# Roots of the norms on ScalarE with scale and epsilon in the same operation, and a spare root ahead of them

## The chip, the core and the metric

The kernel is one program on one core of a Trainium2 chip. The core has a matrix engine (TensorE, PE in the rows), a vector engine (VectorE, DVE), a scalar engine that evaluates functions from tables (ScalarE, ACT), GpSimd (POOL) and SyncE (SP), whose queue issues most of the DMAs. The engines run their own instruction streams and wait for each other by semaphores. The metric is the device time of one execution in microseconds, the median of several runs; lower is better. All data is float32. The engine PE works on operands rounded to a shorter format, so each product is made of three passes: high by high, high by low and low by high.

## What is computed

A stack of three layers. A diffusion-like block of two layers works on 256 latent and 256 context rows of width 1024; a third layer (sparse attention, retention, gated feed-forward) follows on the 256 latent rows. What matters here are the norms:

```python
def rms_norm(x, g):
    y = xf * lax.rsqrt(jnp.mean(xf * xf, axis=-1, keepdims=True) + NORM_EPS)   # 1e-6
    return y * g
...
for i in range(2):
    u = modulate(h, g_pre_mix[i], ...)            # rms_norm(h, gain) * (1 + scale) + shift
    o = even_mixer(u) or odd_mixer(u)             # recurrence + attention, output projection
    h = h + gate * rms_norm(o, g_post_mix[i])
    f = sqrelu_mlp(modulate(h, g_pre_ff[i], ...), w_ff1[i], w_ff2[i])
    h = h + gate * rms_norm(f, g_post_ff[i])
...
yn = (y - mu) * lax.rsqrt(var + GN_EPS) ...       # even layer, per head of 64, GN_EPS = 64e-5
q, k = rms_norm per head of 64                    # odd layer, attention D
o_r = (o - mean) * lax.rsqrt(var + EPS) * w       # third layer, retention, per head of 256
return rms_norm_2(x, norm_final_w)
```

## The kernel before

**The plan.** One Python list, `plan`, is written in the order in which the stages are composed: `step(name, ...)` adds an entry, and generators are advanced in turns to interleave independent work. Then each engine goes through the whole list and emits what it has under each name; an engine that has nothing under a name skips it. So the order on each engine's queue is the order of the plan, and between engines only semaphores order the work (`at(...)` names a point, `wait_ge` waits for points; `ve.last()` and `sc.last()` are the engine's own last instruction). PSUM banks are handed out with `take` and `give`. A queue is in order: what stands behind a waiting instruction waits too.

**Weights.** `cols` declares a chunk of 1 MB: SP loads it into a slot of a ring (L2896), ACT copies it into a window as the rounded high part (`split`, L2448, 128x2048), and DVE subtracts to get the low part (L1869). `chunk` puts the split of each chunk at the place in the plan where the chunk before it was declared, one chunk ahead of its use. PE then multiplies in three passes (L1377 to L1379).

**Norms.** `normed(T, k)` is the norm of tile k (128 rows) in stage T. Its steps: for the norms behind a projection, `residual` (the root of the projected row's mean square, then h + gate * o / rms); `square` (ACT squares and sums H, L2489, with an instruction that reads the accumulator behind it); `diag` (DVE scales and adds epsilon, L1894; ACT takes the root, L2493; DVE takes the reciprocal, L1896, and writes a diagonal matrix, L1901); `x` (PE multiplies the tile by the diagonal, which turns and normalises it, L1442; DVE, L1913 or L1915, and ACT, L2502, copy the result out with gain and shift); `x hi` (ACT, L2448, 128x512) and `x lo` (DVE, L1920). With this the next matrix product can start. The stages are m0 (start), f0 (behind mix0, four tiles), m1 (behind ff2 of layer 0, four tiles), f1 (behind mix1, two tiles), m2 (behind ff2 of layer 1, two), u (third layer, two) and the final norm. A "seam" is the stretch from the end of one product to the start of the next, with such a norm between.

**Projections.** `out_proj` makes the output in two halves of 512 columns, c = 0 and 1. For each half ACT squares and sums the result per tile into `SSQ[:, m, c]` (L2515), and DVE multiplies it by the gate (L1942; L1936 and L1939 where it also adds to an earlier part). In the last chunk of c = 1 the tiles are finished one by one, and the steps of `normed` are advanced, one per generator, between tiles. `residual` on DVE first adds the two sums (L1925), then scales and adds epsilon (L1894), waits for ACT's root (L2493), takes the reciprocal and forms the new h (L1928).

**Other roots.** The recurrence's head norm (`gn var`: DVE L2182 from PSUM, ACT L2643 in place), the query and key norm of the odd layer (`d var`: DVE L2256, ACT L2703), the retention norm (DVE L2368, ACT L2816), the final norm (L1894, L2493), and `prep norm` (L2615), which isn't touched.

A root needs its table on ACT. The load (ACT_TABLE_LOAD) isn't in the source: it is put ahead of the first function whose table isn't the active one, and 36 of them are in the program. Exp, Sigmoid, Silu and Gelu need other tables; Copy, Identity and Square go with any.

## Time and profile before

| | |
|---|---|
| median of 3 runs | 2102.7 us (2098.2 to 2103.3) |
| profiled execution | 2100.6 us, span of its instructions 2098.8 us |
| PE busy | 1863.1 us, 89% |
| weight load of PE busy | 1558.0 us, 74% |
| DVE busy | 1109.6 us, 53% |
| ACT busy | 886.5 us, 42% |
| POOL busy | 214.4 us, 10% |
| chain that ended last | PE 75%, DVE 10%, ACT 6%, issue 2%, POOL 2%, SP queue 2%, DMA 2% |
| mean granted clock of PE | 0.948 of full speed |

The page's chain is to be read as the time that would go if its link were faster: PE's 75% are matrix products, and the 16% of DVE and ACT are links between them. Busy shares of DVE and ACT are averages over stages in which they matter and stages in which they don't.

### The profile page before, as it was taken

The page shows a single profiled execution, that of the slowest core. Times are in us where ns is not written, and L with a number is a line of the kernel's source. Part 1 is how long each engine was busy: PE and PEld are TensorE (multiplying, and loading weights), DVE is VectorE, ACT ScalarE, POOL GpSimd, SP SyncE. Part 2 cuts the span into 40 slices and gives each one's busy share as a digit, 9 for nine tenths or more (in the row PEclk, how much of TensorE's full clock was granted, in tenths as well). Part 3 has the DMA queues.
Part 4 walks back from the last instruction along what each step waited for, and adds up shares of the span by engine and source line. Part 5 has one row for each costly group of instructions (what it writes and reads, how often), then busy time and mean ns, then how long its engine had stood idle before and what let it go on. Part 6 is the DMA issues. An engine that isn't in the chain of part 4 may idle for free.

```text
span 2098.8 us, 40122 instructions
## 1 busy us (share of the span) xinstructions
PE 1863.1 (89%) x16962; PEld 1558.0 (74%) x16962; DVE 1109.6 (53%) x1711; ACT 886.5 (42%) x1423; POOL 214.4 (10%) x214
## 2 busy tenths in 40 slices
PE   5899779888898889999997799799979999679996
PEld 3776568777787688888876676698877677569985
DVE  1457564565545554224344765565445574556863
ACT  2336544353431444214224256564332465346652
POOL 0000035334342000000000100010000000000210
PEclk9999889999999999999998899899989999789998
DMA  8233232222231312233323310365534534134552
GB/s 268 92 121 109 77 121 85 87 91 91 83 103 42 121 61 92 90 100 101 101 80 58 133 61 25 103 186 190 186 108 148 169 98 151 65 124 161 181 163 99
DMA packets 201377, 237.19 MB, mean 113 GB/s; under 512 B 14347, under 2 KB 158573, under 8 KB 201197
## 3 DMA queue, kind: packets, MB, share of 16 engines
q1 hardware_dynamic: 195856, 227.33, 34.2%
q10 hardware_dynamic: 5341, 7.30, 1.0%
q8 instruction: 133, 2.18, 0.4%
q14 instruction: 47, 0.39, 0.1%
HBM read 233.56 MB, written 1.05 MB: 112 GB/s over the span
## 4 chain that ended last, share of the span: by engine, by line
PE 75%; DVE 10%; ACT 6%; issue 2%; POOL 2%; SPq 2%; DMA 2%; ACTq 0%; DVEq 0%; POOLq 0%
PE bank L1377 17%; PE bank L1378 17%; PE bank L1379 17%; PE bank L1569 9%; ACT window L2448 2%; SPq L2896 2%; DVE window L1869 2%; PE bank L1557 2%; PE bank L1536 2%; PE bank L1548 2%; PE bank L1428 1%; PE bank L1442 1%; DVE window L1920 1%; PE bank L1754 1%; PE bank L1576 1%
## 5 line engine op out<-in xcount | busy, mean ns | idle before, releaser
L1377 PE MATMUL bank<-window 128*128 128x512 f32 (+1 forms) x2136 | 762.8, 357 | 55.1 <-DVE window L1920 29.6
L1378 PE MATMUL bank<-window 128*128 128x512 f32 (+1 forms) x2136 | 749.8, 351 | 0.0
L1379 PE MATMUL bank<-window 128*128 128x512 f32 (+1 forms) x2136 | 749.0, 351 | 0.0
L1869 DVE TENSOR_TENSOR window<-arena,window 128x2048 fp32r<-128x2048 f32 (+1 forms) x164 | 372.1, 2269 | 271.5 <-ACT window L2448 269.7
L1377 PEld LDWEIGHTS bank<-window 128*128 128x128 f32 x2136 | 415.5, 195 | 119.0 <-DVE window L1920 30.7
L2448 ACT ACTIVATE window<-arena 128x2048 fp32r<-128x2048 f32 (+3 forms) x292 | 377.1, 1291 | 211.0 <-PE bank L1379 123.5
L1379 PEld LDWEIGHTS bank<-window 128*128 128x128 f32 x2136 | 415.2, 194 | 51.3
L1378 PEld LDWEIGHTS bank<-window 128*128 128x128 f32 x2136 | 416.0, 195 | 48.2 <-issue 0.2
L2448 ACT ACTIVATE arena<-bank 128x256 f32<-128x256 f32 (+1 forms) x298 | 127.0, 426 | 367.1 <-PE bank L1379 128.6
L1569 PE MATMUL bank<-arena 64*64 64x64 f32 (+1 forms) x5888 | 215.2, 228 | 18.8 <-DVE arena L1363 10.2
L1569 PEld LDWEIGHTS bank<-arena 64*64 64x64 f32 x5888 | 201.8, 137 | 35.6 <-DVE arena L1363 11.9
L2842 POOL TENSOR_TENSOR arena<-arena 128x256 f32<-128x256 f32 x80 | 67.8, 848 | 409.9 <-ACT arena L2448 303.6
L2658 ACT ACTIVATE arena<-bank 128x512 f32<-128x512 f32 (+1 forms) x64 | 31.4, 491 | 152.8 <-PE bank L1379 151.5
L2561 ACT ACTIVATE arena<-bank,arena 128x512 f32<-128x512 f32 (+3 forms) x112 | 58.5, 522 | 56.5 <-DVE arena L2016 35.2
L2072 DVE TENSOR_TENSOR arena<-arena,bank 128x512 f32<-128x512 f32 (+1 forms) x80 | 50.7, 634 | 58.8 <-PE bank L1569 57.4
L1442 PE MATMUL bank<-extra,arena 128*128 128x128 f32 x288 | 48.2, 342 | 35.4 <-DVE extra L1901 35.4
L1442 PEld LDWEIGHTS bank<-extra,arena 128*128 128x128 f32 x288 | 46.0, 253 | 38.8 <-DVE extra L1901 38.8
L2210 DVE TENSOR_TENSOR arena<-arena 128x512 f32<-128x512 f32 (+1 forms) x48 | 29.0, 603 | 84.9 <-ACT arena L2658 84.4
L1428 PE MATMUL bank<-arena 128*32 128x256 f32 x768 | 58.8, 426 | 13.3 <-DMA arena<-in_w_ada 13.3
L2016 DVE TENSOR_REDUCE arena<-bank 128x1 f32<-128x512 f32 (+4 forms) x96 | 51.7, 539 | 23.4 <-PE bank L1540 17.0
L2864 POOL TENSOR_TENSOR arena<-arena 128x2048 f32<-128x2048 f32 x2 | 9.0, 4510 | 487.2 <-DMA arena<-in_c_rpb 487.1
L2448 ACT ACTIVATE extra<-bank 128x512 f32<-128x512 f32 (+2 forms) x96 | 46.9, 489 | 19.2 <-PE bank L1548 16.6
(283 smaller groups left out, 1674.8 us busy)
## 6 DMA issues: line engine op xcount, KB each, us to landing
arena<-in_w_ff SPq DMA_DIRECT2D x64, 1024.0 KB, 5.4
arena<-in_w_ada SPq DMA_DIRECT2D x48, 1024.0 KB, 5.6
arena<-in_w_in SPq DMA_DIRECT2D x23, 1024.0 KB, 5.1
arena<-in_w_ffn_up SPq DMA_DIRECT2D x22, 1024.0 KB, 5.0
arena<-in_w_ffn_down SPq DMA_DIRECT2D x10, 1024.0 KB, 5.1
arena<-in_w_in_even SPq DMA_DIRECT2D x9, 1024.0 KB, 5.5
arena<-in_w_out SPq DMA_DIRECT2D x8, 1024.0 KB, 5.2
arena<-in_w_in_odd SPq DMA_DIRECT2D x8, 1024.0 KB, 6.9
```

What stands on the lines that cost most here:

```text
L1377: e.matmul(o, rr(l[0]), rr(r[0]), start=start, stop=False)
L1378: e.matmul(o, rr(l[0]), rr(r[1]), start=False, stop=False)
L1379: return e.matmul(o, rr(l[1]), rr(r[0]), start=False, stop=stop)
L1428: t = e.matmul(u.b[q:q + 32, 0:256], SV[:, k, :], w.v[:, k, :], start=k < 4, stop=k >= 4)
L1442: t = e.matmul(u.b[:, j * 128:j * 128 + 128], H[:, k, (q + j) * 128:(q + j) * 128 + 128], DIAG[:, k, :], start=True, stop=True)
L1569: t = e.matmul(o[h0:h1, c], l[i][h0:h1, c], r[i][h0:h1, c], start=i == 0, stop=i == len(l) - 1)
L1869: e.tensor_tensor(rr(raw), raw, rr(w.high, F32), SUB).then_inc(*ve.tick(w.ready))
L2016: e.tensor_reduce(low[:, h * ns:h * ns + ns], b, AX.X, MAX, negate=True).then_inc(*ve.tick(at("max", S, i, h)))
L2072: e.tensor_tensor(w, w, x, SUB).then_inc(*ve.tick(b.empty, at("w", *u)))
L2448: return e.activation(o, i, ACT.Copy, **k)
L2561: e.activation(a.P[i % a.NP][h][:, s * n:s * n + n], u.b[:, s * n:s * n + n], ACT.Exp, bias=low[:, x:x + 1], accum_out=total[:, x:x + 1]). ...
L2842: return e.tensor_tensor(z.L[l % 2], z.G[:, :, 0], lvl[:, 1 - d, l:l + 1, :].to_broadcast([128, NCH, 64]), MUL)
```

## The change

ACTIVATE computes func(scale * in + bias). The change lets ACT do the scaling and the adding of epsilon inside the root, with scale as an immediate and bias as a column of memory: `eps` (1e-6) and `eps_gn` (64e-5), two columns of `tiny` that DVE sets at the start.

- `square` on ACT is followed at once by the root (`root`), so the root moves from step `diag` to step `square`; DVE's `diag` keeps reciprocal and diagonal.
- `residual`: DVE scales the first half's sum and adds epsilon in `out block` of c = 1 (`first squares`, RS[:, m, 3]); ACT takes the root of the second half's sum with that column as bias. DVE's addition of the sums and its scaling go.
- `gn var`, `d var`, `ret norm` and the final norm: DVE's instruction goes; for the first two ACT reads PSUM itself and frees the bank.
- `root table`: a root of `eps` into a spare column, at the start (behind `silu`, ahead of the loads of h on ACT's queue) and in `out_proj` ahead of c = 1. Where another table is active there, the load stands with it; elsewhere only the spare root is added.

```diff
@@ out_proj
         for c in range(2):
+            if c and (then or not gate):
+                step("root table")
             for m in range(ntok):
@@ start
     step("silu")
+    step("root table")
@@ vector
-        def rstd(acc, var, inv, summed, rooted):
-
-            ve.wait_ge(ve.last(), *([at(*summed)] if summed else []))
-            e.tensor_scalar(var, acc, 1.0 / 1024, 1e-6, MUL, ADD).then_inc(*ve.tick(at("var", *rooted)))
+        def inverse(k, *rooted):
+
             ve.wait_ge(ve.last(), at(*rooted))
-            e.reciprocal(inv, var).then_inc(*ve.tick(at("inv", *rooted)))
+            e.reciprocal(RS[:, k, 2:3], RS[:, k, 1:2]).then_inc(*ve.tick(at("inv", *rooted)))
@@ residual on DVE
-            ve.wait_ge(ve.last(), at("out squares", p.of, k))
-            e.tensor_reduce(RS[:, k, 0:1], SSQ[:, k, :], AX.X, ADD).then_inc(*ve.tick())
-            rstd(RS[:, k, 0:1], RS[:, k, 1:2], RS[:, k, 2:3], None, ("res root", T, k))
+            inverse(k, "res root", T, k)
@@ out_block on DVE
+            if p.gate and c:
+                ve.wait_ge(ve.last(), at("out square", name, 0, m))
+                e.tensor_scalar(RS[:, m, 3:4], SSQ[:, m, 0:1], 1.0 / 1024, 1e-6, MUL, ADD).then_inc(*ve.tick(at("first squares", name, m)))
@@ gn_var and d_var on DVE
-            e.tensor_scalar(pA[:, p, :], u.b[:, :], 1.0 / 64, 64e-5, MUL, ADD).then_inc(*ve.tick(u.empty, at("y var", p)))
-            e.tensor_scalar(TMP[x % 3][:, 0:n], u.b[:, 0:n], 1.0 / 64, 1e-6, MUL, ADD).then_inc(*ve.tick(u.empty, at("d var", x)))
@@ square, residual and root table on ACT
             e.activation(JUNK, H[:, k, :], ACT.Square, accum_out=RS[:, k, 0:1]).then_inc(*sc.tick(at("squared", T, k)))
-
-        def root(a, *key):
-            sc.wait_ge(sc.last(), at("var", *key))
-            e.activation(a, a, ACT.Sqrt).then_inc(*sc.tick(at(*key)))
+            sc.wait_ge(sc.last(), at("eps"))
+            e.activation(RS[:, k, 1:2], RS[:, k, 0:1], ACT.Sqrt, scale=1.0 / 1024, bias=eps).then_inc(*sc.tick(at("root", T, k)))
+
+        def residual(T, k):
+            p = norms[T]
+            sc.wait_ge(sc.last(), at("out squares", p.of, k), at("first squares", p.of, k))
+            e.activation(RS[:, k, 1:2], SSQ[:, k, 1:2], ACT.Sqrt, scale=1.0 / 1024, bias=RS[:, k, 3:4]).then_inc(*sc.tick(at("res root", T, k)))
+
+        def root_table():
+            sc.wait_ge(sc.last(), at("eps"))
+            e.activation(spare_root, eps, ACT.Sqrt).then_inc(*sc.tick())
@@ gn_var and d_var on ACT
-            sc.wait_ge(sc.last(), at("y var", p))
-            e.activation(pA[:, p, :], pA[:, p, :], ACT.Sqrt).then_inc(*sc.tick(at("y root", p)))
+            u = bank("var", p)
+            sc.wait_ge(sc.last(), u.full)
+            e.activation(pA[:, p, :], u.b[:, :], ACT.Sqrt, scale=1.0 / 64, bias=eps_gn).then_inc(*sc.tick(u.empty, at("y root", p)))
-            sc.wait_ge(sc.last(), at("d var", x))
-            e.activation(a, a, ACT.Sqrt).then_inc(*sc.tick(at("d root", x)))
+            u, n = bank("d sums", x), d_parts[x][2]
+            sc.wait_ge(sc.last(), u.full)
+            e.activation(TMP[x % 3][:, 0:n], u.b[:, 0:n], ACT.Sqrt, scale=1.0 / 64, bias=eps).then_inc(*sc.tick(u.empty, at("d root", x)))
```

ACT from the end of mix1's c = 0 to the norm f1, before. L2515 squares the projection, L2448 128x2048 is the split of a chunk, L2493 a root, L2489 the square of h, L2502 the copies of x.

```order
L2515 ACTIVATE extra,arena<-bank 128x512 x2
L2448 ACTIVATE window<-arena 128x2048 x2
L2515 ACTIVATE extra,arena<-bank 128x512
L2493 ACT_TABLE_LOAD
L2493 ACTIVATE arena<-arena 128x1
L2515 ACTIVATE extra,arena<-bank 128x512
L2493 ACTIVATE arena<-arena 128x1
L2489 ACTIVATE extra,arena<-arena 128x1024 x2
L2493 ACTIVATE arena<-arena 128x1 x2
L2502 ACTIVATE arena<-bank,arena 128x128 x8
L2448 ACTIVATE window<-arena 128x4x128 x4
```

The same place after. L2516 is the projection's square, L2442 the split, L2494 the spare root, L2490 the residual's root, L2483 and L2485 the square of h and its root, L2503 the copies of x.

```order
L2516 ACTIVATE extra,arena<-bank 128x512 x2
L2494 ACT_TABLE_LOAD
L2494 ACTIVATE arena<-arena 128x1
L2442 ACTIVATE window<-arena 128x2048 x2
L2516 ACTIVATE extra,arena<-bank 128x512
L2490 ACTIVATE arena<-arena 128x1
L2516 ACTIVATE extra,arena<-bank 128x512
L2490 ACTIVATE arena<-arena 128x1
L2483 ACTIVATE extra,arena<-arena 128x1024
L2485 ACTIVATE arena<-arena 128x1
L2483 ACTIVATE extra,arena<-arena 128x1024
L2485 ACTIVATE arena<-arena 128x1
```

The table load moved from behind the two splits to ahead of them, with the spare root; each root of a norm now stands right behind its square, so that the root of tile 0 is ahead of the square of tile 1.

DVE at the same place, before: L1869 low parts of two chunks, L1942 the gate product, L1925 the sum, L1894 scaling, L1896 reciprocal, L1928 the new h, L1901 a diagonal.

```order
L1869 TENSOR_TENSOR window<-arena,window 128x2048 x2
L1942 TENSOR_TENSOR arena<-bank,arena 128x512
L1925 TENSOR_REDUCE arena<-arena 128x1
L1894 TENSOR_SCALAR arena<-arena 128x1
L1896 RECIPROCAL arena<-arena 128x1
L1928 SCALAR_TENSOR_TENSOR arena<-arena 128x1024
L1942 TENSOR_TENSOR arena<-bank,arena 128x512
L1925 TENSOR_REDUCE arena<-arena 128x1
L1894 TENSOR_SCALAR arena<-arena 128x1
L1896 RECIPROCAL arena<-arena 128x1
L1928 SCALAR_TENSOR_TENSOR arena<-arena 128x1024
L1894 TENSOR_SCALAR arena<-arena 128x1
```

After: L1875 low parts, L1938 the first squares, L1947 the gate product, L1900 reciprocal, L1930 the new h, L1905 a diagonal.

```order
L1875 TENSOR_TENSOR window<-arena,window 128x2048 x2
L1938 TENSOR_SCALAR arena<-arena 128x1
L1947 TENSOR_TENSOR arena<-bank,arena 128x512
L1900 RECIPROCAL arena<-arena 128x1
L1930 SCALAR_TENSOR_TENSOR arena<-arena 128x1024
L1938 TENSOR_SCALAR arena<-arena 128x1
L1947 TENSOR_TENSOR arena<-bank,arena 128x512
L1900 RECIPROCAL arena<-arena 128x1
L1930 SCALAR_TENSOR_TENSOR arena<-arena 128x1024
L1900 RECIPROCAL arena<-arena 128x1
L1905 TENSOR_SCALAR extra<-arena 128x128
L1900 RECIPROCAL arena<-arena 128x1
```

The addition and the scaling between gate product and reciprocal are gone, also the scaling ahead of each diagonal's reciprocal; one scaling of the first half's sum stands ahead of each gate product.

## Rows read from the trace of the kernel before

**Rows 1.** Waits of PE: us in total, times, longest
```profile
PE bank L1442 <- DVE extra L1901: 35.4, 11, 7.5
PE bank L1377 <- DVE window L1920: 29.6, 6, 5.9
```

**Rows 2.** ACT timeline at seam m2: start, duration, line, instruction, idle before
```profile
1522.02 0.60 ACT L2515 ACTIVATE extra<-bank 128x512 f32<-128x512 f32 x1 [6.22 <-PE bank L1379]
1524.74 0.60 ACT L2515 ACTIVATE extra<-bank 128x512 f32<-128x512 f32 x1 [0.56 <-PE bank L1379]
1528.84 1.06 ACT L2489 ACTIVATE extra<-arena 128x1024 f32<-128x1024 f32 x1 [0.50 <-DVE arena L1928]
1530.02 0.20 ACT L2493 ACTIVATE arena<-arena 128x1 f32<-128x1 f32 x1
```

**Rows 3.** DVE timeline at seam m2
```profile
1522.81 0.69 DVE L1942 TENSOR_TENSOR arena<-bank,arena 128x512 f32<-128x512 f32 x1 [4.62 <-ACT extra L2515]
1523.54 0.15 DVE L1925 TENSOR_REDUCE arena<-arena 128x1 f32<-128x2 f32 x1
1523.72 0.15 DVE L1894 TENSOR_SCALAR arena<-arena 128x1 f32<-128x1 f32 x1
1524.28 0.16 DVE L1896 RECIPROCAL arena<-arena 128x1 f32<-128x1 f32 x1 [0.40 <-ACT arena L2493]
1527.46 1.28 DVE L1928 SCALAR_TENSOR_TENSOR arena<-arena 128x1024 f32<-128x1024 f32 x1
1530.32 0.16 DVE L1896 RECIPROCAL arena<-arena 128x1 f32<-128x1 f32 x1 [1.39 <-ACT arena L2493]
```

**Rows 4.** PE timeline at seam m2
```profile
1530.86 6.57 PE L1442 MATMUL bank<-extra,arena 128*128 128x128 f32 x32 [6.22 <-DVE extra L1901]
```

**Rows 5.** Groups of ACT instructions by shape: busy us, mean ns
```profile
L2448 ACT ACTIVATE arena<-bank 128x512 f32<-128x512 f32 x60 | 35.8, 597 | 151.9 <-PE bank L1379 110.4 <-PE bank L1569 24.9 <-PE bank L1451 16.0
L2561 ACT ACTIVATE arena<-bank,arena 128x512 f32<-128x512 f32 x48 | 33.0, 689 | 27.9 <-DVE arena L2016 19.1 <-DVE arena L2019 5.2 <-DVE arena L2021 2.4
```

**Rows 6.** ACT timeline, a table load behind a copy
```profile
1772.71 1.28 ACT L2757 ACT_TABLE_LOAD   x1
1774.00 3.63 ACT L2757 ACTIVATE arena<-arena 128x4096 f32<-128x4096 f32 x1
```

**Rows 7.** ACT and PE timelines in mix1 and seam f1
```profile
1310.59 3.87 ACT L2448 ACTIVATE window<-arena 128x2048 fp32r<-128x2048 f32 x2
...
1320.02 1.28 ACT L2493 ACT_TABLE_LOAD   x1 [1.25 <-DVE arena L1894]
...
1314.49 0.39 PE L1379 MATMUL bank<-window 128*128 128x512 f32 x1
1314.95 0.50 PE L1377 MATMUL bank<-window 128*128 128x512 f32 x1
```

**Rows 8.** DVE and PE timelines at seam f0
```profile
734.97 0.16 DVE L1896 RECIPROCAL arena<-arena 128x1 f32<-128x1 f32 x1 [1.06 <-ACT arena L2493]
...
741.98 0.58 PE L1377 MATMUL bank<-window 128*128 128x256 f32 x1 [4.42 <-DVE window L1920]
```

**Rows 9.** DVE and SP timelines at the end of seam m1
```profile
1123.00 4.32 DVE L1920 TENSOR_TENSOR window<-arena,window 128x512 fp32r<-128x512 f32 x6
...
1127.40 21.74 SPq L2896 DMA_DIRECT2D arena<-in_c_rpb  x32
```

**Rows 10.** Waits of PE from 1188 to 1216 us
```profile
PE bank L1518 <- DVE arena L2266: 1.9, 1, 1.9
PE bank L1377 <- DVE window L1869: 0.9, 1, 0.9
```

**Rows 11.** DVE and ACT timelines, last variance and final norm
```profile
671.43 0.69 DVE L2182 TENSOR_SCALAR arena<-bank 128x512 f32<-128x512 f32 x1 [2.01 <-PE bank L1687]
...
2087.64 1.28 ACT L2493 ACT_TABLE_LOAD   x1 [0.34 <-DVE arena L1894]
```

**Rows 12.** Busy time by stretch, behind seam f0: columns PE PEld DVE ACT POOL, clock
```profile
742.00:750.00 8.00, 8.00 (x44) 8.00 (x45) 5.37 (x7) 2.64 (x3) 0.00 (x0) 0.62 0.00 0
```

More of the change, by code:

```diff
@@ L180, in program @@
     tiny = sb(64)
+    eps, eps_gn, spare_root = [tiny[:, i:i + 1] for i in (63, 62, 61)]
     ident = sb(128)
@@ L2366, in ret_norm @@
         def ret_norm():
-            ve.wait_ge(ve.last(), *[at("ret squared", h, i) for h in range(4) for i in range(2)])
-            e.tensor_scalar(a1, a1, 1.0 / 256, 1e-6, MUL, ADD).then_inc(*ve.tick(at("ret var")))
             ve.wait_ge(ve.last(), at("ret root"))
@@ L2416, in final @@
             a, b, r = [tiny[:, 4 * k + i:4 * k + i + 1] for i in range(3)]
-            rstd(a, b, r, ("final squared", k), ("final root", k))
+            ve.wait_ge(ve.last(), at("final root", k))
+            e.reciprocal(r, b).then_inc(*ve.tick())
             ve.wait_ge(ve.last(), at("spread", ("final",), 0))
@@ L2802, in final @@
             e.activation(junkf, H[:, k, :], ACT.Square, accum_out=a).then_inc(*sc.tick(at("final squared", k)))
-            root(tiny[:, 4 * k + 1:4 * k + 2], "final root", k)
+            sc.wait_ge(sc.last())
+            e.activation(tiny[:, 4 * k + 1:4 * k + 2], a, ACT.Sqrt, scale=1.0 / 1024, bias=eps).then_inc(*sc.tick(at("final root", k)))
         steps = {"load h": load_h, "more columns": more_columns, "silu": silu, "mod": mod, "split": split, "spread": spread,
-                 "square": square, "diag": lambda T, k: root(RS[:, k, 1:2], "root", T, k), "x": norm_x, "x hi": x_hi,
-                 "residual": lambda T, k: root(RS[:, k, 1:2], "res root", T, k), "out block": out_block,
+                 "square": square, "root table": root_table, "x": norm_x, "x hi": x_hi,
+                 "residual": residual, "out block": out_block,
                  "even start": even_start, "kB": kB_, "vB": vB_, "pA": pA_, "pA gates": pA_gates, "scores": scores, "turn p": turn_p,
@@ L2814, in scalar @@
                  "kv": kv_, "vsw": vsw_, "gt": gt_, "gelu": gelu, "vg": vg, "merge start": merge_start, "ret o": ret_o,
[L2815 to L2816 removed]
+                 "ret square": ret_square, "ret norm": lambda: (sc.wait_ge(sc.last()),
+                                                               e.activation(a1, a1, ACT.Sqrt, scale=1.0 / 256, bias=eps).then_inc(*sc.tick(at("ret root")))),
                  "ret turn": ret_turn, "z turn": z_turn_, "up": up, "gated": gated, "final": final,
```

17 lines of the change are left out of this document (5 added, 12 removed).

## The prediction

> **What bounds the kernel now.** I read the page first, then the waits of PE, then the chain of waits, and last the timelines of ACT, DVE and PE at the places where the chain leaves PE. In the waits of PE the reader is to see two releasers ahead of all others: the diagonal that DVE writes from 1/rms, and the low half of the normalised x [rows 1]. Together they cost PE 65 us. They belong to six "seams", places where one matrix product ends and the next can't begin before the rows are normalised: m0 at the start, f0 and m1 with four tiles, f1, m2 and u with two. At a seam the chain runs through ACT and DVE by turns, in instructions of 0.15 to 1.3 us with a hop between engines, so every one that goes from it shortens the kernel. Between seams PE is the bound, and an edit there is worth nothing unless ACT or DVE is late.
>
> **The seam in full: m2, tiles 0 and 1.** Before: ACT squares tile 0 at 1522.02 [rows 2]; DVE multiplies by the gate until 1523.50, adds the two sums (1523.54), scales and adds epsilon (1523.72), waits 0.40 us for the root, takes the reciprocal at 1524.28 [rows 3]. After: root 0 stands behind its own square on ACT (0.68 us for square and accumulator read, then the root), done at 1523.0 beside the gate product, so the reciprocal follows at 1523.53: 0.75 us earlier. Tile 1's square is released by PE at 1524.74 [rows 2] and doesn't move; its reciprocal comes behind the gate product at about 1526.24, the residual product (1.28 us) ends at 1527.72 instead of 1528.74. DVE has one small instruction more there, the first squares (0.15 us as the scaling of the same shape, with a gap 0.19), but it lies in the wait for that square.
> The order gives more than the removed instructions. Before, ACT does square 0, square 1, root 0, root 1; root 0 starts at 1530.02, behind square 1 which waited for the second residual, and DVE idles 1.39 us before reciprocal 0 [rows 2, 3]. After, root 0 follows square 0 and is done near 1527.2. Reciprocal and diagonal of tile 0 then wait only for DVE's own residual product: 1527.75 + 0.19 + 0.29 = 1528.23, PE starts at 1528.28 and not at 1530.86 [rows 4]. That is 2.6. Tile 1's diagonal is ready near 1529.8, before PE has done tile 0's sixteen matmuls (half of 6.57 us [rows 4]), so PE doesn't stop again. Less 0.25 for the spare root of this projection: **2.3 us**.
>
> **Price of the new forms.** No root of before has a bias from memory. ACTIVATE on 128x512 from PSUM is 597 ns as a copy and 689 ns with such a bias [rows 5], so I add 0.09 us to each root (0.20 to 0.29); from below it is 0, from above 0.1. The Trainium skill, page "ScalarE: Activation LUTs", section "What ACT_TABLE_LOAD costs", says each [128,1] pointer operand adds about 93 ns; by that rule, the trace agrees, and it speaks mildly against the change, which gives 42 roots such an operand. A table load takes 1.28 us; where one stands right behind a copy (no idle time is put before it, at 1772.71) the next ACTIVATE begins at 1774.00, nothing between [rows 6]. So a spare root with its load is 1.28 + 0.20 + two gaps = **1.54 us** of ACT, one without load 0.25. The same section puts a drain of about 1380 ns on each switch; the rows show none, and if it appeared where a load is moved to, f1 would be worth 1.4 us less.
> The loads stay as many as they were (36); three are moved: at m0, before mix1's second half, before down's second half.
>
> **f1 (behind mix1).** The same walk as m2 gives its 2.6, and the load of 1.28 us, which stands at 1320.02 between the scaling and root 0 with nothing beside it [rows 7], is gone from there: 3.9 us. But the load isn't gone. It now stands on ACT in front of the split of 1310.59, and that split is itself on the chain: PE finished the chunk before it and started at 1314.95, 0.46 us behind the start of the last matmul where 0.23 is the rule [rows 7]. No slack, so all 1.54 us come back as a wait of PE. Net **2.4**. What is queued behind the load: two splits, the second for the first feed-forward chunk, which has the whole seam as slack.
>
> **f0 and m1 (four tiles).** By the same walk the residual products come 0.75 us earlier at tile 0 and 0.55 more for each further tile (0.74 less the 0.19 of the first squares, which here stand between busy DVE instructions). Then the order: at f0 DVE waits 1.06 us for the last root, which stands on ACT behind copies of x and splits, and all low halves come behind it [rows 8]. After, tile 0's diagonal is ready at 721.95, PE takes 3.7 us for its sixteen matmuls, and from 725.7 on ACT runs without a gap: copies of x of tile 0 (1.93), square and root of tile 3 (1.5, done at 729.1), copies of tile 1, high half of tile 0 (1.29), copies of tile 2, high half of tile 1, which ends at 735.7; DVE, no longer held by the root, has tile 1's low half ready at 736.5, and PE starts there and not at 741.98: 5.4. At m1 the last low halves end at 1127.3 (1123.00 + 4.32), and SP starts the 32 loads of the bias right behind, 21.7 us ahead of the weights of the odd layer [rows 9]; so m1's end passes to all that follows through SP. After, by the same walk (tile 0's diagonal at 1102.1, tile 1's at 1106.6, ACT without a gap from 1110.2), ACT's last high half ends at 1121.4 and DVE at 1122.1: 5.2. Lower end of each is the removed instructions alone, 0.74 + 3 x 0.55 + 0.25 = 2.6. A four-tile walk has many joints, so I take **5.0 and 4.9**.
>
> **Query and key norm of the odd layer.** The variance leaves DVE. Its last two instructions stood on DVE behind a copy that waits for a matrix product, while ACT sat idle; ACT now takes those roots straight from PSUM, and the split queued behind them comes earlier too, as do DVE's low half and reciprocals. PE has two waits there that hang on it, 0.9 and 1.9 us [rows 10]: both go, **2.8**, from below 0 if the copy or the weights hold the split anyway.
>
> **The rest.** u: root 0 before square 1: **1.1**, from the same order. Recurrence: the last variance, 0.69 us on DVE with nothing beside it [rows 11], is taken by ACT: **0.7**; the other three lie in a stretch where PE is busy: 0 to 2.1, I take 0.5. Retention norm: a hop and a small instruction, **0.2**. Final norm: the load of 1.28 us goes from the end of the kernel [rows 11] and two hops of 0.24; its spare root stands before a split with about 1.0 us of slack, so 0.5 comes back: **1.3**. m0: the chain runs on loads of w_ada and w_in_even; four roots earlier are hidden by them: 0; the spare root stands ahead of the loads of h, which are wanted 20 us later.
>
> **Sum.** 2.3 + 2.4 + 5.0 + 4.9 + 2.8 + 1.1 + 0.7 + 0.5 + 0.2 + 1.3 = 21.2. The profiled execution took 2100.6 (span 2098.8), so 2079.4; the median of the runs shown lies 2.1 above it: **2081.5 us**, 1.0% faster. Its own range: with the odd layer at 0 and f0 and m1 half way to their lower ends it is 2087; with all of the recurrence's 2.1, the full walks and a little clock it is 2076.
>
> **Rivals.**
> A. Only the removed instructions count, since at each seam the next thing (ACT's copies of x, a split, PE's own slow matmuls) is late in the place of the root. Then f0 and m1 give 2.6 each, f1 1.2, m2 1.3, u 0.25, the odd layer 0, final 1.3, the rest 0.9: 10 us, **2092**. For it: ACT is nearly full in the second half of f0 and m1. Against: at m2 and f1 both engines stand idle for over 1 us, waiting for that root [rows 2, 3].
> B. The seams become short enough that PE's clock isn't lowered behind some of them. After f0's seam, in which PE was mostly idle, the granted clock was 0.62 over 8 us: the lower level, 1.2 GHz, for most of it [rows 12], some 3.0 us lost. Spared at three of the five seams: **2073**. Against: at m2 PE would still be idle for some 3.6 us, and most of the time behind that.
> C. Slower. Four lanes share DVE's, ACT's and POOL's queues in the recurrence (245 to 645 us). Three instructions fewer on DVE move the phase of the lanes, and each of the 16 units could find one engine taken. The gains elsewhere are paid back if a unit loses 1.3 us (21.2/16); at 1.9 us, 30 us are lost: **2112**. It is one mechanism, but a queue that is emptier usually lets the next in sooner, and DVE is busy only a good half of the time there, by the page's slices.
> D. The change doesn't do what it says: the moved loads hurt at mix1 and down, the seams keep their length because the trace's hops are shorter with the new waits than I think: **2100**.
>
> **Chances.** Forecast 0.62, A 0.23, B 0.08, C 0.03, D 0.04. A measurement of this kernel tells some 0.3% (6 us) from no change: faster 0.93, within it 0.04, slower 0.03. The range holds the forecast's own and reaches to A and B: 2073 to 2094.
>
> **What would show it.** In the trace after: each root at 0.29 us right behind its square; PE's waits for the diagonal and the low half down from 65 to some 45 us; at mix1 a table load before a split and a new wait of PE for the low half of weights near 1.5 us; no load in the last 12 us; SP's bias loads starting some 12 us earlier by the span; no wait of PE for the key norm. I am wrong if m1's end moves less than 3 us against m1's start, if the recurrence's length changes by more than 3 us, or if PE's first matmul behind a seam is released by something new.

## The result and the profile after

The changed kernel takes 2072.9 us (median of 4 runs, 2072.2 to 2077.4) against 2102.0 us before: ratio 0.987, 95% interval 0.9857 to 0.9883. That is 29 us, 1.3 to 1.4% faster, where the forecast was 2081.5 us and its range 2073 to 2094. The direction and most of the waits were as forecast, but the time is 8.6 us below the forecast and stands at the lower end of the range (0.1 us under it). Of the 8.6, 7.0 are missing in the sum (28.2 us gained by the spans, 21.2 forecast); the other 1.6 come from the medians, which lay 2.1 us above the profiled execution before and 0.5 after. The profiled span went from 2098.8 to 2070.6 us, and its mean granted clock from 0.948 to 0.954.

The waits of PE, after (us in total, times, longest). The diagonal (line 1905 now) holds PE for 18.0 us instead of 35.4, the low half of x (line 1924) for 28.8 instead of 29.6 [rows 1]. Together that is 46.8 where 45 was expected. The third row, the low half of weights (L1875), was 16.6 before, and the new wait at mix1 is in it.

```profile
PE bank L1381 <- DVE window L1924: 28.8, 6, 5.7
PE bank L1381 <- DVE window L1875: 19.0, 9, 5.0
PE bank L1446 <- DVE extra L1905: 18.0, 9, 4.4
```

Seam m2 on ACT, answering to [rows 2]: start, duration, line, instruction, idle before. L2516 is the square of the projection, L2490 the residual's root, L2483 and L2485 the square of h and its root, L2503 the copies of x.

```profile
1500.64 0.60 ACT L2516 ACTIVATE extra<-bank 128x512 f32<-128x512 f32 x1 [6.22 <-PE bank L1383]
1501.14 0.19 ACT L2516 ACTIVATION_READ_ACCUMULATOR extra<-bank 128x1 f32 x1
1501.36 0.29 ACT L2490 ACTIVATE arena<-arena 128x1 f32<-128x1 f32 x1
1503.36 0.60 ACT L2516 ACTIVATE extra<-bank 128x512 f32<-128x512 f32 x1 [1.70 <-PE bank L1383]
...
1504.41 1.06 ACT L2483 ACTIVATE extra<-arena 128x1024 f32<-128x1024 f32 x1
1505.37 0.19 ACT L2483 ACTIVATION_READ_ACCUMULATOR extra<-arena 128x1 f32 x1
1505.59 0.29 ACT L2485 ACTIVATE arena<-arena 128x1 f32<-128x1 f32 x1
1506.45 1.06 ACT L2483 ACTIVATE extra<-arena 128x1024 f32<-128x1024 f32 x1 [0.57 <-DVE arena L1930]
```

Each root takes 0.29 us and stands right behind its square. Root 0 (1505.59) is ahead of square 1 (1506.45), where before it stood behind it. On DVE, answering to [rows 3], nothing is left between gate product (L1947) and reciprocal (L1900), and the 1.39 us of idle time before reciprocal 0 are gone:

```profile
1504.15 0.69 DVE L1947 TENSOR_TENSOR arena<-bank,arena 128x512 f32<-128x512 f32 x1 [0.32 <-ACT extra L2516]
1504.88 0.16 DVE L1900 RECIPROCAL arena<-arena 128x1 f32<-128x1 f32 x1
1505.08 1.28 DVE L1930 SCALAR_TENSOR_TENSOR arena<-arena 128x1024 f32<-128x1024 f32 x1
1506.39 0.16 DVE L1900 RECIPROCAL arena<-arena 128x1 f32<-128x1 f32 x1
1506.59 0.29 DVE L1905 TENSOR_SCALAR extra<-arena 128x128 f32<-128x128 f32 x1
```

PE, answering to [rows 4]: the wait is 3.67 us instead of 6.22, which is the 2.6 of the walk. But the 32 matmuls themselves now take 5.28 us instead of 6.57, and nothing was removed from them:

```profile
1506.93 5.28 PE L1446 MATMUL bank<-extra,arena 128*128 128x128 f32 x32 [3.67 <-DVE extra L1905]
```

The same line by its instructions, over seams f1 and m2, of before and then of after. The three numbers are the shortest, the median and the longest duration in ns:

```profile
L1442 PE MATMUL bank<-extra,arena x64: 275/421/582, 1328.2 to 1537.2; 128*128 128x128 f32 x64
```
```profile
L1446 PE MATMUL bank<-extra,arena x64: 274/306/579, 1308.1 to 1511.9; 128*128 128x128 f32 x64
```

The matmuls that lasted 275 ns ran at the higher clock level; at the lower one most lasted some 420, and the 580 are the first ones behind a wait. What counts for the time is how far apart they start: 0.21 us at the lower level (24 of them in 5.12 us from 1531.45 on, before) and 0.11 at the higher (12 in 1.33 us from 1510.05 on, after). The granted clock over the 32 was 0.56 before and 0.71 after. This is the part that the forecast's sum left out.

mix1 after, on ACT and then on PE. The spare root's load (L2494) stands ahead of two splits, and PE gets a wait of 1.30 us that [rows 7] don't have:

```profile
1292.80 1.28 ACT L2494 ACT_TABLE_LOAD   x1
1294.10 0.20 ACT L2494 ACTIVATE arena<-arena 128x1 f32<-128x1 f32 x1
1294.33 3.86 ACT L2442 ACTIVATE window<-arena 128x2048 fp32r<-128x2048 f32 x2
...
1298.70 0.50 PE L1381 MATMUL bank<-window 128*128 128x512 f32 x1 [1.30 <-DVE window L1875]
```

The other places: PE's first feed-forward product of f0 (answers to [rows 8]); SP's loads of the bias, 12.0 us earlier than in [rows 9]; ACT's root of the last variance straight from PSUM, and the last root of the kernel, which has no load before it (both answer to [rows 11]).

```profile
735.74 0.58 PE L1381 MATMUL bank<-window 128*128 128x256 f32 x1 [4.42 <-DVE window L1924]
...
1115.39 20.08 SPq L2899 DMA_DIRECT2D arena<-in_c_rpb  x30
...
671.76 0.69 ACT L2645 ACTIVATE arena<-bank,arena 128x512 f32<-128x512 f32 x1 [1.28 <-PE bank L1691]
...
2065.67 0.30 ACT L2806 ACTIVATE arena<-arena 128x1 f32<-128x1 f32 x1
```

**Where the time went.** Both kernels issue the same 16962 matmuls in the same order, so the start of the i-th can be taken from either trace and subtracted. What is gained in a stretch has two parts: PE waits less (no matmul runs), or the same matmuls take less time, which is how TensorE's clock shows. Over the whole kernel the second part is the difference of PE's busy time, 1863.1 us before and 1859.6 after. "with fillers" is the gain between two kernels of the experiments with filler matmuls in their seams (below). The stretches end at 671, 713, 1090, 1167, 1300, 1515, 1700 and 2000 us of the trace before. In us gained:

| stretch | forecast | measured | of it waits | of it matmul time | with fillers |
|---|---|---|---|---|---|
| recurrence | 0.5 | -0.3 | 2.0 | -2.3 | 0.9 |
| last variance | 0.7 | 0.7 | 0.7 | -0.1 | 0.7 |
| f0 | 5.0 | 7.1 | 4.1 | 3.1 | 5.7 |
| m1 | 4.9 | 4.9 | 6.1 | -1.1 | 5.4 |
| odd layer's key and query norm | 2.8 | 5.1 | 2.8 | 2.3 | 3.9 |
| mix1 and f1 | 2.4 | 3.9 | 2.8 | 1.1 | 3.9 |
| m2 | 2.3 | 5.3 | 3.4 | 1.8 | 4.0 |
| retention, u | 1.3 | 0.3 | 1.3 | -1.0 | 0.9 |
| down, final norm | 1.3 | 1.3 | 1.6 | -0.3 | -0.1 |
| sum | 21.2 | 28.2 | 24.7 | 3.5 | 25.3 |

The waits of down and final norm hold the 2.1 us gained behind the last matmul. (The ends of matmuls are modelled in the profile, so the split into the two parts is less sure than their sum.) The repetition of the changed kernel has nearly the same waits in most places (m2 2.6, m1 5.7, the others within 0.5) but other matmul times at f1 (-0.2) and m2 (4.3): the clock's part of a single seam differs by 1 to 2.5 us between two traces of the same code, its sum outside the recurrence less (5.8 us here, 7.0 in the repetition).

The recurrence scatters from trace to trace by more than the change could do there: up to its last matmul the delay against before was 0.3 us in the first trace of the changed kernel, 0.7 in its second, -0.4 in a variant that leaves the recurrence's code alone, and 1.5 in another. Its -2.3 us of matmul time can't be laid to the change of its variances, since the kernel with these put back has -2.5.

### The profile page after: what moved, and what is told of

It is laid out like the page before. It is cut to its first block, busy times and chain, and to the rows that moved or that the text cites. A ratio compares the mean times of both kernels' runs of the same rounds, so it can differ in the third digit from the quotient of the medians.

```text
span 2070.6 us, 40061 instructions
## 1 busy us (share of the span) xinstructions
PE 1859.6 (90%) x16962; PEld 1554.9 (75%) x16962; DVE 1097.0 (53%) x1671; ACT 892.2 (43%) x1430; POOL 214.7 (10%) x214
## 4 chain that ended last, share of the span: by engine, by line
PE 77%; DVE 9%; ACT 5%; POOL 2%; SPq 2%; issue 2%; DMA 2%; ACTq 0%; DVEq 0%; POOLq 0%
PE bank L1381 18%; PE bank L1383 17%; PE bank L1382 17%; PE bank L1573 9%; ACT window L2442 2%; SPq L2899 2%; DVE window L1875 2%; PE bank L1561 2%; PE bank L1540 2%; PE bank L1552 2%; PE bank L1432 1%; PE bank L1446 1%; PE bank L1758 1%; PE bank L1580 1%; PE bank L1544 1%
## 5 line engine op out<-in xcount | busy, mean ns | idle before, releaser
L1381 PE MATMUL bank<-window 128*128 128x512 f32 (+1 forms) x2136 | 761.0, 356 | 56.6 <-DVE window L1924 28.8
L1875 DVE TENSOR_TENSOR window<-arena,window 128x2048 fp32r<-128x2048 f32 (+1 forms) x164 | 372.1, 2269 | 273.5 <-ACT window L2442 271.7
L2442 ACT ACTIVATE window<-arena 128x2048 fp32r<-128x2048 f32 (+3 forms) x292 | 377.1, 1291 | 209.8 <-PE bank L1383 121.7
L2442 ACT ACTIVATE arena<-bank 128x256 f32<-128x256 f32 (+1 forms) x298 | 127.3, 427 | 368.6 <-PE bank L1383 130.1
L2442 ACT ACTIVATE extra<-bank 128x512 f32<-128x512 f32 (+2 forms) x96 | 47.0, 489 | 19.4 <-PE bank L1552 16.8
```

What stands on the lines that cost most here:

```text
L1381: e.matmul(o, rr(l[0]), rr(r[0]), start=start, stop=False)
L1875: e.tensor_tensor(rr(raw), raw, rr(w.high, F32), SUB).then_inc(*ve.tick(w.ready))
L2442: return e.activation(o, i, ACT.Copy, **k)
```

## The experiments

All kernels of one comparison ran on the same chip, with runs of the kernel before among them (medians 2100.8 to 2101.7).

**The changed kernel again**, as the base of the first comparison.

> The changed kernel once more, as the yardstick of this call. Both theories: 2073 us, ratio to the kernel before 0.987; f0's first feed-forward matmul about 7 us earlier than in the kernel before, the odd layer's key norm about 5 us.

Measured: 2072.4 us, ratio 0.9861 (0.9846 to 0.9876), span 2071.1. The gain repeats, with 5.9 us at f0's first product (about 7 expected) and 5.3 in the odd layer.

**Root of the square back behind the next square** (the new form, the old order).

```diff
             e.activation(JUNK, H[:, k, :], ACT.Square, accum_out=RS[:, k, 0:1]).then_inc(*sc.tick(at("squared", T, k)))
+
+        def root(T, k):
             sc.wait_ge(sc.last(), at("eps"))
...
-                 "square": square, "root table": root_table, "x": norm_x, "x hi": x_hi,
+                 "square": square, "diag": root, "root table": root_table, "x": norm_x, "x hi": x_hi,
```

> The changed kernel with each square's root put back behind the next square (same instruction forms, same number, old place in ACT's order). Theory 1 (the order on ACT is a large part of the gain): slower than the changed kernel by 1.6 us at f1 and m2 each, 0.9 at u, 2 to 3 at f0 and m1 each, 9 us in all, plus 2 to 3 us where PE's lower clock stretches come back: 2082 to 2085. Theory 2 (only the removed instructions count): within 1 us of the changed kernel.

Measured: 2083.0 us, ratio 0.9903 (0.9887 to 0.992), 10.6 above the control. PE's wait for the diagonal is back at 27.6 us:

```profile
PE bank L1381 <- DVE window L1924: 29.2, 6, 5.7
PE bank L1446 <- DVE extra L1905: 27.6, 11, 5.3
```

So over a third of the gain is the place of an instruction in ACT's queue and not the instructions saved, within theory 1's 2082 to 2085. By stretch, against the trace of the changed kernel, it is 2.5 us at f0, 0.8 at m1, 3.1 at mix1 and f1, 4.0 at m2 and 0.2 at u, where theory 1 had 1.6 at f1 and m2 each and 2 to 3 at m1. It is a matter of waits: between matmuls PE stands idle 11.7 us longer than in the changed kernel, and its matmul time is the same within half a microsecond.

**Residual's sum, scale and epsilon back on VectorE.**

```diff
-    e.activation(RS[:, k, 1:2], SSQ[:, k, 1:2], ACT.Sqrt, scale=1.0 / 1024, bias=RS[:, k, 3:4])
+    e.tensor_reduce(RS[:, k, 0:1], SSQ[:, k, :], AX.X, ADD)                       # DVE
+    e.tensor_scalar(RS[:, k, 1:2], RS[:, k, 0:1], 1.0 / 1024, 1e-6, MUL, ADD)     # DVE
+    e.activation(RS[:, k, 1:2], RS[:, k, 1:2], ACT.Sqrt)                          # ACT
```

> The changed kernel with the residual's root as before (addition, scaling and epsilon on DVE, no first squares). Theory 1: 0.74 us at the first tile of a seam and 0.55 at each further one come back, 2.4 at f0 and m1, 1.3 at f1 and m2, 7.4 us in all, 2080. Theory 2 (this part carries nearly all of the gain at the seams, with its clock): 12 us or more, 2085.

Measured: 2080.3 us, ratio 0.9898 (0.9883 to 0.9913), 7.9 above the control, in the time of theory 1. That the time fits is partly luck: by stretch this kernel loses 3.3 us at f0, 1.6 at m1, 2.4 at mix1 and f1 and 3.7 at m2 against the trace of the changed kernel, 11.0 where theory 1 had 7.4, and gains 3.3 at u, where its matmuls ran faster (below). Each part of the norms, taken out alone, costs several microseconds: neither covers for the other.

**Spare root one half earlier.**

```diff
-            if c and (then or not gate):
-                step("root table")
...
             if c == 0:
+                step("root table")
                 for m in range(ntok):
                     step("out block", name, c, m)
```

> The changed kernel with the spare root ahead of the squares and copies of the first half instead of ahead of the second half, where ACT waits for PE 5 to 6 us. Theory 1 (the spare root with its load stands before a split on the chain): PE's wait of 1.3 us in mix1 and the 1.0 us lost in down go, 2.2 us faster than the changed kernel, 2071. Rival (the split has slack, the loss comes from elsewhere): no change, 2073.

Measured: 2068.6 us (2066.9 to 2072.0), ratio 0.9845 (0.983 to 0.9859), 3.7 below the control where theory 1 had 2.2 and its rival 0. The interval overlaps the control's, and the profiled execution, the slowest of the four, is only 0.9 us shorter than the control's; the trace is clearer at the two places. mix1's start no longer loses anything (the delay changes there by 0.05 us instead of 1.2) and the end of down loses nothing instead of 0.8.

**No spare roots in the output projections.**

```diff
-            if c and (then or not gate):
-                step("root table")
```

> The changed kernel without its spare roots between an output projection's halves (out_proj; the one in the recurrence's prologue stays). Each load of the root's table (1.28 us) is then back in front of the residual's first root: at f1 and in the final normalisation on the path, and away from mix1's start and from down. Theory 1 (a load is moved, and it costs where it stands only if ScalarE is waited for there): mix1's start comes 1.2 us earlier than in the changed kernel, f1's first feed-forward matmul loses that and another 0.1 to 1.3, the end of down gains 0.7 to 1.0 and the final normalisation loses 1.3: together within 1.5 us of the changed kernel, 2072 to 2074, with each step seen at its place. Theory 2 (the load ahead is a real saving, of its whole duration at each seam): two loads of 1.28 and a drained pipeline each, 2075.5 to 2077.

Measured: 2069.6 us, ratio 0.9851 (0.9836 to 0.9865): 2.7 to 3.2 us below the changed kernel and its repetition. Neither theory had that. ACT in mix1 and f1 shows why:

```profile
1299.56 0.60 ACT L2514 ACTIVATE extra<-bank 128x512 f32<-128x512 f32 x1 [3.63 <-PE bank L1381]
1300.06 0.19 ACT L2514 ACTIVATION_READ_ACCUMULATOR extra<-bank 128x1 f32 x1
1300.27 1.28 ACT L2488 ACT_TABLE_LOAD   x1
1301.56 0.30 ACT L2488 ACTIVATE arena<-arena 128x1 f32<-128x1 f32 x1
1302.28 0.60 ACT L2514 ACTIVATE extra<-bank 128x512 f32<-128x512 f32 x1 [0.42 <-PE bank L1381]
```

Before, the load came behind a wait for DVE's scaling [rows 7]. With the root right behind its square it falls into time in which ACT waits for PE's next product, 1.70 us at the same place in the changed kernel. It still has 0.42 us to spare. PE's wait for f1's first diagonal becomes 3.2 us shorter than before instead of 3.8, presumably through DVE's residual product, which needs this root. So the load ahead brings 0.6 us at f1 and costs 1.2 at mix1. In the final norm it brings its 1.3 (there the load stands in the chain, 2056.52 us in this trace) and costs 0.8 in down. The rest is at u: from 1810 to 1898 us this kernel gains 3.1 against before and the changed kernel 0.1. That is hardly the spare roots' doing, since the kernel with the residual's sum on VectorE has them all and gains 3.3 there; it is taken up below.

**Key and query norm's scale and epsilon back on VectorE.**

```diff
+    e.tensor_scalar(TMP[x % 3][:, 0:n], u.b[:, 0:n], 1.0 / 64, 1e-6, MUL, ADD)    # DVE "d var"
-    e.activation(TMP[x % 3][:, 0:n], u.b[:, 0:n], ACT.Sqrt, scale=1.0 / 64, bias=eps)
+    e.activation(a, a, ACT.Sqrt)
```

> The changed kernel, with the scale and epsilon of the odd layer's key and query norm back on VectorE (a tensor_scalar from PSUM ahead of the root). Theory 1 (the step is worth what the waits were, and also the stretch of lower TensorE clock that stood behind them): PE's two waits of 1.9 and 0.9 us of rows 10 come back, and the stretch at 1209 runs again at the lower clock: 4.3 to 5.2 us slower than the changed kernel, 2076.5 to 2077.6, with the granted clock near 1209 below 0.8. Theory 2 (waits alone): 2.8 us, 2075. Theory 3 (those waits went because other work came earlier by the layer's start): 0 to 1 us, 2072 to 2073.5.

Measured: 2079.2 us, ratio 0.9891 (0.9876 to 0.9905), 6.3 above the changed kernel, and in the traces 4.6 of it lie between 1160 and 1217 us. Both waits of PE are back at their old length [rows 10]. The second fence is a stretch of 10 us behind them, with columns as in [rows 12]; the changed kernel has 1.00 there.

```profile
PE bank L1522 <- DVE arena L2266: 1.9, 1, 1.9
PE bank L1381 <- DVE window L1875: 0.9, 1, 0.9
```
```profile
1196.00:1206.00 10.00, 10.00 (x50) 8.21 (x49) 6.28 (x11) 3.68 (x6) 0.00 (x0) 0.86 0.28 105
```

2.8 us of waits cost 4.6 us of time. Theory 1 names the mechanism, though its clock (below 0.8) and its time (2077.6 at most) weren't met; the other 1.6 us lie behind 1328 us, in seams that this edit doesn't touch.

**Recurrence's variances back on VectorE.**

```diff
+    e.tensor_scalar(pA[:, p, :], u.b[:, :], 1.0 / 64, 64e-5, MUL, ADD)            # DVE "gn var"
-    e.activation(pA[:, p, :], u.b[:, :], ACT.Sqrt, scale=1.0 / 64, bias=eps_gn)
+    e.activation(pA[:, p, :], pA[:, p, :], ACT.Sqrt)
```

> The changed kernel, with the scale and epsilon of the recurrence's output variances back on VectorE. Theory 1 (only the last variance stands on the path): the step from the last variance to mix0's start loses 0.7 to 0.8 us and the 340 us of the recurrence's pairs before it gain or lose nothing beyond 0.5: 2072.5 to 2074. Theory 2 (VectorE's time counts in the recurrence: all four variances cost): 2 to 3 us, 2074.5 to 2076. Theory 3 (the changed order cost the recurrence the 0.35 us that the matmul at 670 lies later): it comes back, and the sum is within 0.4 us of the changed kernel.

Measured: 2073.9 us, ratio 0.9867 (0.9852 to 0.9882), in the time of theory 1. The step from the last variance to mix0 is 0.0 us in this trace and 0.74 to 0.75 in every trace of the new form that was matched here. The recurrence is as long as in two traces of the new form. The last variance counts; the other three give nothing that stands out of the recurrence's scatter.

**Fillers.** Short matmuls of the identity where PE waits in seams m1, f1, m2, u and ahead of five products behind seams, nine places in all. The text below also names down; no filler stands there.

```diff
+        def warm(u, n):
+            pe.wait_ge(u.before)
+            for _ in range(n):
+                e.matmul(u.b[:, 0:128], ident, ident, start=True, stop=True)
+    # (abridged) normalising, k == 0 and q == 0, in m1, f1, m2, u: warm(u, 16)
+    # first ff1 of f0: 24; first qD: 24; first qN: 32; first up: 32; ff1 of f1: 32
```

> The changed kernel, with 16 to 32 short matmuls (128 columns of the identity, into the bank that the next product overwrites) put where TensorE waits in the seams: 16 ahead of the first tile's sums in m1, f1, m2 and u, 24 or 32 ahead of the first feed-forward, receptance, down and up products. They compute nothing that is used. Theory 1 (part of what the change gained beyond its waits is TensorE's clock, lowered after idle stretches, and the clock can be held up by any work): the granted clock behind the seams (724 to 750, 1109 to 1150, 1306 to 1325, 1504 to 1523) is 0.9 or more, and 4 to 10 us are gained: 2063 to 2069, although a filler that is still running delays the product behind it by up to 1 us at each place. Theory 2 (the clock is lowered for another reason, or PE waits in the seams for VectorE and ScalarE anyway, so that a faster clock there only waits longer): within 1.5 us of the changed kernel. Theory 3 (fillers stand in the way): each seam 1 us later, 2077 to 2082.

Measured: 2066.0 us, ratio 0.9828 (0.9812 to 0.9845). The kernel does more work and is 6 to 7 us faster, as theory 1 had it. Seam f1 without the fillers and with them (columns: width, PE busy, granted clock, DMA share, GB/s):

```profile
1285.00:1330.00 45.00, 34.32 (x189) 0.92 0.36 106
```
```profile
1285.00:1330.00 45.00, 43.60 (x300) 1.00 0.37 118
```

**The same fillers in the kernel before.** This asks how much of the 29 us is the clock. The places are nine, not eight as that text says.

```diff
+    # (abridged) the kernel before, with warm(u, n) at the same places and of the same numbers
```

> The kernel before, with the same filler matmuls of TensorE at the same eight places as in the kernel with fillers on the changed one (2066.0 us in its own comparison). With the clock held up in both, the difference of the two is what the change takes out of the chains alone. Theory 1 (the change gained 29 us because its waits are 21 to 23 us shorter and TensorE's clock is lowered behind its seams for 7 us less): this kernel gains more from the fillers than the changed one did (6.4), namely 9 to 15 us: 2087 to 2092, and stands 21 to 25 us above the changed kernel with fillers. Theory 2 (the steps of the forecast are each worth more than put down, and the clock is a bystander): the fillers gain the same 5 to 7 us here, 2094.5 to 2097, and the difference stays 29 us.

Measured: 2090.3 us, ratio 0.9953 (0.9939 to 0.9966). The fillers bring 10.5 us here against 6.4 in the changed kernel, and the two stand 24.3 us apart (25.3 by the spans, 26.3 by the ratios), against 28 to 29 without fillers (27.3 and 29.2 by the ratios). Both of theory 1's times are met, and its mechanism holds: part of the gain is TensorE's clock. But the distance of these two kernels isn't the gain without the clock, for the fillers don't hold it up equally in both. The matmuls that are common to both still take 5.6 us less in the changed kernel with fillers. At m2's 32 normalising matmuls the granted clock is 0.67 in the kernel before with fillers and 1.00 in the changed one (columns as in [rows 12]):

```profile
1528.00:1533.20 5.20, 4.99 (x30) 4.99 (x31) 2.47 (x9) 1.42 (x5) 0.00 (x0) 0.67 0.00 0
```
```profile
1505.00:1509.00 4.00, 3.90 (x35) 3.86 (x35) 2.60 (x9) 2.58 (x7) 0.00 (x0) 1.00 0.35 91
```

So the clock's size is read from the matmul times of the two kernels without fillers (the table above). Seams f1 and u of this kernel, and in the second fence those of the kernel before:

```profile
1305.00:1350.00 45.00, 40.99 (x279) 0.96 0.36 113
...
1860.00:1900.00 40.00, 39.39 (x308) 1.00 0.32 106
```
```profile
1305.00:1350.00 45.00, 31.53 (x165) 0.85 0.32 96
...
1865.00:1905.00 40.00, 30.48 (x193) 0.83 0.31 100
```

**Fillers, no spare roots but one in down, ahead of its first half's blocks.**

```diff
-            if c and (then or not gate):
-                step("root table")
...
             if c == 0:
+                if name == "down":
+                    step("root table")
```

> The changed kernel with the fillers, without the spare roots between the halves of the output projections, and with one spare root of down moved ahead of its first half's blocks, where ScalarE is not waited for. Theory 1 (a load costs only where ScalarE is late, and the fillers make the clock's part of the seams the same for every order): against the kernel with fillers mix1's start gains 1.2, f1 loses 1.3, down gains 0.7 to 1.0: 2064.5 to 2066. Theory 2 (the spare roots cost more than they bring, 2.7 us by the kernel without them): 2062 to 2064.

Measured: 2061.5 us, ratio 0.9819 (0.9803 to 0.9836): theory 1 missed by 3 us, theory 2 by half a microsecond.

**The same with fewer fillers.**

```diff
-    warm(u, 16)    -    ff1 of f0: 24    -    ff1 of f1, first qN, first up: 32
+    warm(u, 12)    +    ff1 of f0: 16    +    ff1 of f1, first up: 24    (qN stays 32)
```

> The kernel of the run before with fewer fillers: 12 instead of 16 ahead of the normalising, 16 instead of 24 at f0's feed-forward and the key product, 24 instead of 32 at f1's, at the receptance and at up. Theory 1 (a filler that still runs when its product could start delays it; at f0 the first product came 1 us later with fillers than without): 1 to 2 us faster than with the full number, as long as the clock behind the seams stays at 1.0. Theory 2 (fewer fillers let the clock fall again): 2 to 5 us slower than with the full number, granted clock below 0.95 in one of the seams.

Measured: 2055.5 us (2050.6 to 2058.2), ratio 0.9784 (0.9768 to 0.98), the lowest median of all versions: 17 us below the changed kernel. (That text says 24 for the receptance and 16 for the key product; the kernel kept 32 and 24 there.) Against the run before it is 6.0 faster, in theory 1's direction but beyond its 1 to 2; by the two traces it is 3.3, of which 1.2 lie in the recurrence, ahead of every filler. The seam u:

```profile
1828.00:1868.00 40.00, 39.59 (x300) 1.00 0.32 107
```

**Fewer still.**

```diff
-    warm(u, 12)    -    ff1 of f0: 16    -    ff1 of f1, first qD, first up: 24    -    first qN: 32
+    warm(u, 8)     +    ff1 of f0: 8     +    ff1 of f1, first qD, first up: 16    +    first qN: 24
```

> The kernel with fewer fillers (2055.5 us), with fewer still: 8 instead of 12 ahead of the normalising, 8 instead of 16 at f0's feed-forward, 16 instead of 24 at the key product, f1 and up, 24 instead of 32 at the receptance. Theory 1 (fillers still run into their product at the other places): another 0.5 to 2 us faster, 2053.5 to 2055, with the granted clock at 1.0 in the seams of f0, f1 and u. Theory 2 (the idle time left open between fillers and product is now long enough for the clock to fall): 2 to 5 us slower, 2057 to 2061, with one of the seams below 0.95.

Measured: 2062.5 us (2058.6 to 2063.5), ratio 0.9811 (0.9797 to 0.9824), 7 us slower: the direction of theory 2, beyond its 2057 to 2061. The granted clock fell below 1.00 at f0 and f1, where it is 1.00 in the same stretches of the version before (f0, then f1):

```profile
724.00:760.00 36.00, 31.94 (x214) 0.95 0.17 54
...
1300.00:1330.00 30.00, 25.87 (x193) 0.89 0.27 86
```

That this makes the 7 us isn't shown. The two profiled executions are only 1.3 us apart (spans 2057.7 and 2056.4), and all of that lies in the recurrence, ahead of every filler: behind it the two take the same time within 0.1 us, since this kernel loses 1.3, 3.0 and 3.3 us at f0, f1 and m2 and gains 5.1 at m1 and 2.8 between m2 and u. They also ran on different chips, in comparisons of their own.

## Why the prediction was right, and where it was short

- **The seam in full (m2, 2.3).** The walk was right to 0.05: PE's first normalising matmul comes 2.55 us earlier against the end of the product before it, forecast 2.6, and the run with the root back in its old place loses most of it. That PE doesn't stop again among the 32 was right too, and its wait for the low half behind them is 5.35 us before and after, so the second tile's chain gave nothing of its own. What failed is to end the sum there. Another 2.8 us were gained behind the walk: 1.3 inside the 32 matmuls (6.57 to 5.28 us) and 0.6 in the products behind them, both matmul time, and 0.9 in a wait for the low half of weights (2.3 to 1.4 us), which in the repetition is back at 2.3 while the matmul time there is larger.
- **Price of the new forms.** 0.09 us for the bias was right: the groups give 294 and 295 ns where a spare root has 203. A load follows the instruction before it at once and the next follows the load at once (1300.27, 1.28 us, then 1301.56 in the kernel without spare roots). The drain that the Trainium skill, page "ScalarE: Activation LUTs", section "What ACT_TABLE_LOAD costs", puts on each switch is in none of the rows read here.
- **f1 (net 2.4).** The cost at mix1 was near (1.54 forecast, 1.30 as a wait and 1.2 in the matched starts). Walk plus load, 3.9, came as 3.8 in PE's wait for the first diagonal, but the two terms were wrong and made up for each other: the run without spare roots shows that the new order alone, load in place, brings 3.2 and not 2.6, because it hides half of the load's 1.28. The moved load is worth 0.6 and costs 1.2. That 5.1 came in all is the matmul time behind it, 1.0 us, of which the repetition shows nothing (-0.3).
- **f0 and m1 (5.0 and 4.9).** f0's first product came 5.8 us earlier against mix0's start (walk 5.4), but 1.6 of it are the normalising matmuls at a better clock and only 4.3 are waits, so the walk was too long by 1.1 and the clock made it good. Another 1.4 followed right behind it, where [rows 12] had 0.62 of clock. The changed kernel has 0.79 in the same 8 us:

```profile
735.00:743.00 8.00, 7.26 (x50) 7.27 (x51) 6.09 (x8) 5.23 (x7) 0.00 (x0) 0.79 0.00 1
```

  m1 is 4.9 as forecast, 6.1 of waits less 1.1 of matmul time, and its end passed through SP as said: 12.0 us earlier, of which 7.5 had come from before m1. That m1's gain agrees with its forecast is in part luck, for the waits gave more and the forecast had no term for the clock.
- **Key and query norm (2.8).** The waits went as said, and the expected 2.8 was all of them. The step that failed is to stop there: a wait of PE costs its own length and the slower matmuls behind it. From 1200 to 1217 us the gain was 4.8 for 2.8 of waits, and the other 2.1 are matmul time; it is so in every trace of the new form that was matched here, and the run with the key and query variances back loses both.
- **The rest.** Last variance 0.7: measured 0.74 and confirmed by taking it back. The other three: 0, not 0.5. Final norm and down 1.3: measured 1.3 (2.1 at the end, 0.8 back in down). Retention 0.2 and u 1.1: 0.3 together. The chain gave what was forecast: PE's waits are 1.3 us shorter. The matmul time took it back, 1.0 us more than before (granted clock 0.83 over the 40 us of u before and 0.83 after). In the two variants that gain 3.1 and 3.3 from 1810 to 1898 us the waits are 1.6 shorter and the matmul time 1.7 and 1.9. Why the clock came out so differently there isn't known.
- **Rivals.** A (only removed instructions count) is out: the order alone is worth 10.6 us. B was given 0.08 and taken as an alternative to the forecast; it is in truth a term of the same sum. Its 2073 us is the measured time, but by luck: it had 9 us of clock on top of 21.2, and there were 3.5 in all, 5.8 outside the recurrence, not at three seams of 3.0 each but spread (f0 3.1, odd layer 2.3, m2 1.8, f1 1.1, and back at m1 and u); the rest of the gap was filled by waits and by where the medians lay. C and D are out.

The sum of the causes: 21.2 as forecast, 3.5 more of waits (24.7 in all) and 3.5 of matmul time, which makes 28.2. Without the recurrence, whose two parts are scatter as far as the traces tell, the waits gave 22.7 where 20.7 were forecast (21.4 in the repetition) and the clock 5.8 (7.0 in the repetition). So the waits were forecast well in sum (f0 too long by 1 us, m1 and m2 too short by as much), the term that was put at nothing is the clock, and how it is split over the seams stays open within 1 to 2.5 us a seam.

## What to carry to other kernels

Where engines hand a small chain back and forth, look at the order in each queue before the count of instructions: moving a root ahead of the next square was worth a third of the gain. Price two edits of one chain together, since a load that one edit hides can't be saved again by the other. And a wait of TensorE that is removed can give back more than its length when slower matmuls stood behind it (2.8 us of waits, 4.8 of time in the odd layer), or less (1.3 of waits, 0.3 of time at u), so put the clock into the sum as a term and not among the rivals. A time that comes out as forecast doesn't show that its terms did: compare waits and matmul time one by one.

## What the runs showed of the hardware

- The 128x128 f32 matmuls of the norms start 0.11 us apart at the higher level (2.4 GHz; each lasts 275 ns) and 0.21 apart at the lower (1.2 GHz; some 420 ns, and up to 582 right behind a wait). The lower level was seen behind stretches in which PE waited, and filler matmuls whose results are never used kept the granted clock at 1.00 in seams f1 and u of the best version, where it was 0.85 and 0.83 before and 0.92 and 0.83 in the changed kernel. They don't do so everywhere: 0.67 at m2 in the kernel before with fillers.
- How many fillers are best isn't settled: 16 to 32 each took 2061.5 us, 12 to 32 took 2055.5 and 8 to 24 took 2062.5, but behind the recurrence the traces of the last two are equally long.
- An ACT_TABLE_LOAD of 1.28 us cost 1.2 us ahead of a split that PE was waiting for, and 0.6 at f1, where it stood behind a square in time in which ACT waits for PE.
